# A hybrid attention and convolution layer in float32: four of 17 blocks of the product with V taken from rounded parts, and what moves with them

## The chip, the core and the metric

One core of a Trainium2 chip runs the whole layer in one launch. The metric is the device time of a run in microseconds, and a run is compared by its median. Engines are named as in the profile: PE (TensorE) with PEld (its weight loads), DVE (VectorE), ACT (ScalarE), POOL (GpSimd) and SP (SyncE, which here only issues DMAs).

## What is computed

The reference is one layer of a diffusion backbone: 2048 sample tokens (each attends to the 2048 sample keys and to 128 cached ones) and 128 prompt tokens, width 1024, four attention heads. What matters here is the attention of the sample tokens:

```python
s = jnp.einsum('bqhmd,bkhmd->bhmqk', qblk, k) * scale    # two maps m per head
p = jax.nn.softmax(s, axis=-1)
a = p[:, :, 0] - lam * p[:, :, 1]                        # 2176 keys = 17 blocks of 128
out = jnp.einsum('bhqk,bkhe->bqhe', a, v)                # v: 128 wide per head
```

Before it stand a normalization, adaLN modulation and one wide projection (q, k, v, gates, convolution branches), after it a gated normalization and the output projection.

## The kernel before

**Two kinds of matmul.** PE takes operands of type float32 or float32r. A float32r operand has to be a rounded value, so where the kernel wants float32 accuracy from it, it splits a number into a rounded high part and the remainder ("hi" and "lo") and makes three products, hi\*hi, hi\*lo and lo\*hi. The projections, the scores (`scores`, L926) and the output projection (`out_half`, L1087) work so. The transposes (`transposes`, L981) and the product with V (`product`, L989) take float32 operands. In the trace a float32 matmul of the product is two MATMUL records with a weight load each.

**Stages.** Projections (to about 780 us, the last ones being the convolution branches of four channel groups, `conv_unit`, in which POOL has nothing to do), the attention (about 830 to 1478 us), the output projection.

**The attention's steps.** One step belongs to one tile of 128 queries of one head; there are NT = 64. All four engines walk through the same numbered steps in loops of four (`Fori`, the first 8 or 16 written out), each in its own fixed order, and are held together by semaphores only. Work on one tile is spread over later steps: scores, maxima and exponentials of tile n in step n, its denominators and the combination of the two maps in step n + 1, its transposes in step n + 2, their last evacuation in step n + 3, the product with V in steps n + 4 and n + 5, for two tiles at a time, because the product takes 256 columns.

- PE, step n (four parts p = 0..3): scores of one of four pieces; in p = 1 and p = 2 also the last 384 keys of one map; the product of an earlier pair (`product`: half 0, nine key blocks, in even steps, half 1, eight blocks, in odd ones); four transposes of tile n - 2.
- DVE, step n: p = 0: maximum of 1024 scores (L1856), evacuation of four transposed blocks (keys 12 to 15) of tile n - 3 (`tr_dve`, L1823), then the denominators of tile n - 1: a multiplication of six numbers (L1874), a sum (L1878) and a reciprocal (L1882). p = 1: maximum of 768 scores and of 384 (`max_third`, L1842). p = 2: maximum of 1024, then `combine` (L1830), which adds the two maps over the first 1024 keys. p = 3: maxima of 384 and 768, and the smallest of them (`both_maxima`, L1742).
- ACT, step n: the exponentials (L1376, L1344), the scaling of the second map's first 1024 keys (`scale_first`, L1337; it waits for POOL's coefficients), the evacuation of the other transposed blocks (L1312), the product's result (`att_out`, L1320), and factors for the denominators (L1353).
- POOL, tile n (`factors`): two small multiplications that make the coefficients (L758, which waits for the reciprocal, and L760), six multiplications of 384 keys (L764 and L767 in turn), two additions of 576 keys (L773).

In steps 6 to 13 DVE also makes the low parts of the output weights (`wo_lo`, L1815), one per step, at the end of p = 1. At the start, DVE finishes the last convolution group inside step 1 (L1640 to L1662).

The kernel before calls the product with this wait in front of half 1: `pe.wait_ge(t_dve, n - 3)`.

Of the kernel before, what the change touches and what calls it, by code (L numbers as in the profile page):

```python
# [30 lines left out]
P = 128  # L31
# [6 lines left out]
H = 4  # L38
# [22 lines left out]
TGROUPS = [(0, 4), (4, 4), (8, 4), (12, 4), (16, 1)]  # L61
PIECES = [(0, 1024), (1024, 1792), (1792, KEYS)]
# [19 lines left out]
def hymba_layer(nc, a):  # L82
# [3 lines left out]
    for name, shape in (("k", [H, 2, P, KCOLS]), ("q", [H, 2, P, T]), ("v", [H, P, TILES, P]),  # L86
                        ("ga", [H, P, T]), ("cv", [H, 2, P, T]), ("att", [H, P, T])):
        spill[name] = nc.dram_tensor(f"spill_{name}", shape, F32, kind="Internal").ap()

    ctx = ExitStack()  # L90
    with ctx:
# [32 lines left out]
        with ExitStack() as ectx:  # L124
            qsl = sb("qsl", [P, 2, GW], F32R, ectx)
            blkr = sb("blkr", [P, P], F32R, ectx)
        cb = sb("cb", [P, D])
# [34 lines left out]
        with ExitStack() as bctx:  # L162
            kb = sb("kb", [P, 2, 2, KEYS], F32R, bctx)
            qb = sb("qb", [P, 4, 2, 2, P], F32R, bctx)
            sb("epad", [P, P], F32, bctx)
            e1 = sb("e1", [P, 2, KEYS], F32, bctx)
            e0 = sb("e0", [P, 4, KEYS], F32, bctx)
            with ExitStack() as kctx:
                kp = sb("kp", [P, H, T], F32R, kctx)
            at = sb("at", [P, 2, KT, 2 * P], F32, bctx)  # L170
            vb = sb("vb", [P, KT, P], F32, bctx)
            atto = sb("atto", [P, 2, 2 * P], F32, bctx)
            sb("spad", [P, 12 * 8 + 8 * H], F32, bctx)
            worw = sb("worw", [P, 2, DJ, P], F32, bctx)
            with ExitStack() as pctx:
                sb("vpad", [P, 6 * H * P], F32, pctx)
                sb("qpad", [P, 9 * H * P - P], F32, pctx)
                qp = sb("qp", [P, 2, 2 * H, P], F32R, pctx)
            wo = sb("wo", [P, DJ, 2, DJ, P], F32R, bctx)

# [165 lines left out]
        t_dve = sem("t_dve")  # L346
        pv_mm = sem("pv_mm")
# [39 lines left out]
        def f32(ap):  # L387
            return ap.bitcast(F32)
# [31 lines left out]
        def _(sp):  # L420
# [103 lines left out]
            def load_v(head, part):  # L524
                j0, j1 = (0, 9) if part == 0 else (9, KT - 1)
                sp.dma_start(vb[:, j0:j1], spill["v"][head, :, j0:j1]).then_inc(s_v[part], 16)
                if part == 1:
                    sp.dma_start(vb[:, KT - 1], a["cache_v"][:, head * P:(head + 1) * P]).then_inc(s_v[part], 16)
# [26 lines left out]

            def store_conv(f, tg):
                c0, c1 = behind(tg)
                sp.wait_ge(cvc, 4 + 6 * (NG * f + tg) + 6)
                for hl, src in ((0, chi), (1, clo)):
                    sp.dma_start(spill["cv"][f, hl, :, c0:c1], src[:, 0:c1 - c0]).then_inc(stored, 16)  # L560
# [6 lines left out]
            for f in range(H):  # L567
                c = CVC + CV * f
                for tg in range(NG):
# [7 lines left out]
                    if tg < 3:  # L577
                        for i in range(GATE_CUT[f] + 2 * tg, min(GATE_CUT[f] + 2 * tg + 2, GATE_CUT[f + 1])):
                            load_gate(i)
                    sp.wait_ge(z_used, CV0 + CV_UNITS * f + CV * tg + 1)  # L580
                    sp.dma_start(spill["ga"][f, :, c0:c0 + n], gs[:, 0:n]).then_inc(aux_stored, 16)
                    if tg == 3 and f + 1 < H:
                        sp.wait_ge(g_done, GATE_CUT[f + 1])
                        load_w(c + 5, 0)
                        load_w(c + 6, 1)
# [31 lines left out]
            load_q(3, 0, 3 * P)  # L617
            load_v(0, 0)
# [87 lines left out]
        def _(pool):  # L706
# [39 lines left out]
            qk_unit(H, 0, unit=False)  # L746

# [36 lines left out]
        def _(pe):  # L784
# [199 lines left out]
            def product(b, half, part):  # L984

                js = (range(0, 9), range(9, KT))[half]
                cut = (0, 2, 4, 6, 9) if half == 0 else (0, 2, 4, 6, 8)
                for i in range(cut[part], cut[part + 1]):
                    mm = pe.matmul(ps[:, 7, b * 2 * P:(b + 1) * 2 * P], vb[:, js[i]], at[:, b, js[i], :],  # L989
                                   start=(half == 0 and i == 0), stop=(half == 1 and i == len(js) - 1))  # L990
                if part == 3:
                    mm.then_inc(pv_mm, 1)

            def step(it, t, sc=True, tr=True, tr_last=True, pv=True):
                n = 4 * it + t
                for p in range(4):
# [18 lines left out]
                    if pv:  # L1015
                        half = t % 2
                        b = t // 2
                        if p == 0:
                            pe.wait_ge(s_v[half], (32 if half else 16) * ((it + 3) // 4))
# [449 lines left out]
        def _(dve):  # L1469
# [347 lines left out]
            def tr_dve(n, t):  # L1817

                j0, cnt = TGROUPS[3]
                dve.wait_ge(t_mm, 5 * n + 4)  # L1820
                if t % 2 == 0:
                    wait(dve, pv_mm, n - 2)
                dve.tensor_copy(at[:, t // 2, j0:j0 + cnt, (t % 2) * P:(t % 2 + 1) * P],  # L1823
                                trbank(3).rearrange("p (j q) -> p j q", j=cnt)).then_inc(t_dve, 1)
# [20 lines left out]
            def step(it, t, sc=True, den=True, comb=True, tr_last=True):  # L1845
                n = 4 * it + t
                b = t % 2
                for p in range(4):
# [23 lines left out]
                    if p == 0 and den:  # L1872
# [3 lines left out]
                    if p == 0 and den:  # L1876
# [3 lines left out]
                    if p == 0 and den:  # L1880
# [178 lines left out]
```

## Time and profile before

| what | value |
|---|---|
| runs | 1669.56 us median of 3 (1669.47 to 1671.62) |
| profiled execution | 1670.42 us, span 1668.6 us, granted clock 0.992 |
| PE busy | 1629.1 us (98%) |
| DVE, ACT, POOL busy over the span | 1018.3 (61%), 873.2 (52%), 765.5 (46%) |
| attention steps, 1000 to 1200 us: DVE, ACT, POOL busy | 167.83, 179.19, 186.55 of 200 us |

How to read it: the busy shares over the span mix stages with very different loads (POOL has no work at all in the convolution stage). A PE that is shown as busy need not be at its peak, since its matmuls overlap in the records: how fast it goes is seen from the distance between the starts of its matmuls. Lines are those of the kernel before.

### The profile page before, as it was taken

How to read it: one execution, taken by the hardware profiler on the slowest of the kernel's cores; microseconds unless marked ns; L12 is line 12 of the kernel's file. 1: busy time of each engine (PE TensorE's matmuls, PEld its weight loads, DVE VectorE, ACT ScalarE, POOL GpSimd, SP SyncE). 2: the span in 40 equal slices, each digit the busy share in tenths (PEclk: the TensorE clock that was granted, in tenths of full speed). 3: DMA queues.
4: the chain of work that ended last, by engine and by line, in shares of the span. 5: the costliest groups of instructions: out<-in, count | busy, mean ns of one | idle time of the engine just before them, and what ended most of it. 6: DMA issues, size and time to landing. Idle time of an engine off the chain costs nothing.

```text
span 1668.6 us, 25622 instructions
## 1 busy us (share of the span) xinstructions
PE 1629.1 (98%) x8476; PEld 1460.1 (88%) x8476; DVE 1018.3 (61%) x1613; ACT 873.2 (52%) x1827; POOL 765.5 (46%) x807
## 2 busy tenths in 40 slices
PE   4999999999999999999989999999999999999999
PEld 2888999999999999999968888888888888889999
DVE  4553666663343344333389988888888888745442
ACT  4664666640010100100279989989889898823320
POOL 0002898960000000000079999999999999800000
PEclk8999999999999999999979999999999999999999
DMA  9662323342131231124152223113211211265441
GB/s 366 221 206 101 120 101 110 112 145 84 58 108 54 71 107 53 59 68 121 40 132 87 84 51 93 38 35 85 64 31 35 65 31 50 76 211 182 177 158 49
DMA packets 127232, 168.47 MB, mean 101 GB/s; under 512 B 10816, under 2 KB 113728, under 8 KB 126272
## 3 DMA queue, kind: packets, MB, share of 16 engines
q1 hardware_dynamic: 122032, 163.19, 30.3%
q10 hardware_dynamic: 5136, 4.46, 0.8%
q8 instruction: 36, 0.59, 0.2%
q14 instruction: 28, 0.23, 0.0%
HBM read 117.54 MB, written 50.07 MB: 100 GB/s over the span
## 4 chain that ended last, share of the span: by engine, by line
PE 85%; DMA 4%; DVE 3%; ACT 3%; SPq 2%; issue 2%; POOL 1%; DVEq 0%; POOLq 0%; ACTq 0%
PE ps L808 39%; PE ps L926 14%; PE ps L989 13%; PE ps L1087 11%; PE ps L981 7%; DMA scr<-in_xtok 1%; DMA raw<-in_w_in 1%; DMA xt<-in_xtok 1%; DVE stt L1856 1%; DMA out_y<-yo 1%; ACT scr L1175 1%; SPq L535 1%; PE ps L860 0%; PE ps L861 0%; SPq L430 0%
## 5 line engine op out<-in xcount | busy, mean ns | idle before, releaser
L808 PE MATMUL ps<-hT,w 128*128 128x448 f32 (+1 forms) x3360 | 677.3, 361 | 0.3 <-DVE w L1500 0.3
L808 PEld LDWEIGHTS ps<-hT,w 128*128 128x128 f32 x3360 | 621.7, 188 | 48.2 <-DVE w L1500 1.1
L926 PE MATMUL ps<-kb,qb 128*128 (+2 forms) x1276 | 321.3, 381 | 8.5 <-ACT e L1376 4.0
L1856 DVE TENSOR_REDUCE stt<-ps 128x1 f32<-128x1024 f32 x252 | 273.6, 1086 | 58.8 <-PE ps L926 58.4
L1376 ACT ACTIVATE e<-ps,stt 128x1024 f32<-128x1024 f32 x252 | 255.6, 1014 | 61.1 <-DVE stt L1856 54.6
L989 PE MATMUL ps<-at,vb 128*128 128x256 f32 x1088 | 276.7, 381 | 0.8 <-ACT atto L1320 0.5
L758 POOL TENSOR_TENSOR stt<-stt,lamc 128x2 f32<-128x2 f32 x64 | 12.5, 195 | 505.8 <-DVE stt L1882 505.8
L926 PEld LDWEIGHTS ps<-kb,qb 128*128 128x128 f32 x1276 | 217.8, 192 | 26.5 <-issue 7.1
L989 PEld LDWEIGHTS ps<-at,vb 128*128 128x128 f32 x1088 | 199.0, 190 | 29.0 <-ACT atto L1320 3.2
L764 POOL TENSOR_TENSOR e<-e,stt 128x384 f32<-128x384 f32 x192 | 212.5, 1107 | 5.0
L1282 ACT ACTIVATE scr<-ps 128x448 f32<-128x448 f32 (+1 forms) x40 | 20.9, 532 | 311.5 <-PE ps L808 311.5
L773 POOL TENSOR_TENSOR e<-e 128x576 f32<-128x576 f32 x128 | 180.7, 1430 | 0.0
L981 PE MATMUL ps<-cst,e 128*128 128x128 f32 x1088 | 172.3, 275 | 2.2 <-DVE e L1830 0.7
L767 POOL TENSOR_TENSOR e<-e,stt 128x384 f32<-128x384 f32 x192 | 173.7, 905 | 0.0
L981 PEld LDWEIGHTS ps<-cst,e 128*128 128x128 f32 x1088 | 137.6, 142 | 35.4 <-issue 3.5
L1312 ACT ACTIVATE at<-ps 128x512 f32<-128x512 f32 (+1 forms) x256 | 131.6, 515 | 9.4 <-PE ps L981 9.4
L727 POOL TENSOR_TENSOR qx<-qx,scr 128x448 f32<-128x448 f32 (+1 forms) x40 | 45.2, 1129 | 169.8 <-DVE qx L1597 165.7
L808 PE MATMUL ps<-w,hT 128*128 128x512 f32 x408 | 97.5, 399 | 8.2 <-DVE hT L1550 8.1
L1830 DVE SCALAR_TENSOR_TENSOR e<-e,stt 128x1024 f32<-128x1024 f32 x64 | 90.4, 1413 | 19.5 <-ACT e L1337 19.5
L1087 PE MATMUL ps<-mixa,wo 128*128 128x448 f32 (+1 forms) x480 | 101.1, 360 | 0.0
L1087 PE MATMUL ps<-mixc,wo 128*128 128x448 f32 (+1 forms) x480 | 100.9, 360 | 0.0
L808 PEld LDWEIGHTS ps<-w,hT 128*128 128x128 f32 x408 | 77.5, 192 | 25.2 <-DVE hT L1550 7.8
(161 smaller groups left out, 1751.8 us busy)
## 6 DMA issues: line engine op xcount, KB each, us to landing
raw<-in_w_in SPq DMA_DIRECT2D x32, 512.0 KB, 4.4
qb<-spill_q SPq DMA_DIRECT2D x256, 64.0 KB, 2.3
scr<-in_xT SPq DMA_DIRECT2D x8, 1024.0 KB, 6.1
raw<-in_w_gate SPq DMA_DIRECT2D x16, 512.0 KB, 4.4
spill_k<-scr SPq DMA_DIRECT2D x32, 224.0 KB, 2.2
spill_q<-scr SPq DMA_DIRECT2D x32, 224.0 KB, 2.2
mixc<-spill_cv SPq DMA_DIRECT2D x8, 896.0 KB, 7.9
xr<-in_xT SPq DMA_DIRECT2D x4, 1792.0 KB, 13.2
```

Source lines behind the costliest of these rows:

```text
L764: pool.tensor_tensor(e1[:, b, k0:k1], e1[:, b, k0:k1], stt[:, b, 7, 3 + c:4 + c].to_broadcast([P, k1 - k0]), ALU.mult)\
L767: pool.tensor_tensor(e0[:, t, k0:k1], e0[:, t, k0:k1], stt[:, b, 7, c:c + 1].to_broadcast([P, k1 - k0]), ALU.mult)\
L773: add = pool.tensor_tensor(e0[:, t, k0:k1], e0[:, t, k0:k1], e1[:, b, k0:k1], ALU.add)
L808: mm = pe.matmul(out, slot_of(l, j), rhs_of(r, j), start=(i == 0 and j == 0), stop=(i == 2 and j == DJ - 1))
L926: mm = pe.matmul(out[:, c0 - k0:c1 - k0], qb[:, t, ver, m], keys, start=(ver == 0), stop=(ver == 1))
L981: mm = pe.transpose(trbank(g)[:, i * P:(i + 1) * P], e0[:, t, (j0 + i) * P:(j0 + i + 1) * P], ident)
L989: mm = pe.matmul(ps[:, 7, b * 2 * P:(b + 1) * 2 * P], vb[:, js[i]], at[:, b, js[i], :], start=(half == 0 and i == 0), stop=(half == 1 and ...
L1087: mm = pe.matmul(ps[:, k % 4, 0:n], wo[:, o, l, j + H * (1 - half)], part[:, r, j, 0:n], start=(half == 0 and i == 0 and j == 0), stop=(ha ...
L1312: act.activation(at[:, t // 2, j0:j0 + cnt, (t % 2) * P:(t % 2 + 1) * P], trbank(g).rearrange("p (j q) -> p j q", j=cnt), ACT.Copy).then_i ...
L1376: act.activation(dst[:, PIECES[c][0]:PIECES[c][1]], pair(c), ACT.Exp, bias=stt[:, b, 0, 3 * m + c:3 * m + c + 1], accum_out=stt[:, b, 1, 3 ...
L1830: dve.scalar_tensor_tensor(e0[:, t, k0:k1], e0[:, t, k0:k1], stt[:, t % 2, 7, 0:1], e1[:, t % 2, k0:k1], ALU.mult, ALU.add).then_inc(a_rea ...
L1856: dve.tensor_reduce(stt[:, b, 0, 3 * m + c:3 * m + c + 1], pair(c), AX.X, ALU.max, negate=True).then_inc(mx_done, 1)
```

## The change

Three things change together.

1. The product with V takes key blocks 12 to 15 (SB0 = 12, SB = 4) from rounded parts: three float32r matmuls of 256 columns in place of one float32 matmul. DVE's evacuation of these blocks writes the rounded high part `ath` instead of `at`, and a second instruction subtracts it from the transposed block in PSUM into the low part `atl`. The order of the blocks changes (HALVES), so that all four lie in half 0, and PE's wait for DVE's evacuation moves to p = 2 of half 0. `atl` has one buffer, so the evacuation of the next pair waits for one more product (`pv_mm`).
2. V's parts are made in the last channel group of the convolution stage: per head one load of four blocks, POOL's copy (high) and subtraction (low), two stores. In the attention, a head's V comes as four DMAs and a small one instead of two and a small one.
3. The denominators (L1874, L1878, L1882) move in DVE's order from p = 0 to p = 1, behind the second maximum and `max_third`, in front of `wo_lo`.

```diff
+SB0, SB = TGROUPS[3]
+HALVES = ([0, 1, 2, 3, 12, 4, 13, 14, 15], [5, 6, 7, 8, 9, 10, 11, 16])
+CUTS = ((0, 2, 4, 6, 9), (0, 2, 4, 6, 8))
...
             def load_v(head, part):
-                j0, j1 = (0, 9) if part == 0 else (9, KT - 1)
-                sp.dma_start(vb[:, j0:j1], spill["v"][head, :, j0:j1]).then_inc(s_v[part], 16)
...
+                if part == 0:
+                    sp.dma_start(vb[:, 0:5], spill["v"][head, :, 0:5]).then_inc(s_v[0], 16)
+                    for hl in range(2):
+                        sp.dma_start(f32(vhl[:, hl]), spill["vs"][hl, head]).then_inc(s_v[0], 16)
+                else:
+                    sp.dma_start(vb[:, 5:SB0], spill["v"][head, :, 5:SB0]).then_inc(s_v[1], 16)
+                    sp.dma_start(vb[:, KT - 1], a["cache_v"][:, head * P:(head + 1) * P]).then_inc(s_v[1], 16)
...
+            def load_parts(head):
+                if head == 0:
+                    sp.wait_ge(g_done, GATE_CUT[H])
+                    for i in range(2):
+                        sp.wait_ge(v_stored[i], 16 * ((TILES + 1 - i) // 2))
+                wait(sp, vs_stored, 32 * head)
+                sp.dma_start(vraw[:], spill["v"][head, :, SB0:SB0 + SB]).then_inc(vs_in, 16)
+
+            def store_parts(head):
+                sp.wait_ge(vs_lo, head + 1)
+                for hl in range(2):
+                    sp.dma_start(spill["vs"][hl, head], f32(vhl[:, hl])).then_inc(vs_stored, 16)
...
+                    if f == H - 1 and tg < H:
+                        load_parts(tg)
                     sp.wait_ge(z_used, CV0 + CV_UNITS * f + CV * tg + 1)
                     sp.dma_start(spill["ga"][f, :, c0:c0 + n], gs[:, 0:n]).then_inc(aux_stored, 16)
+                    if f == H - 1 and tg < H:
+                        store_parts(tg)
...
+            for head in range(H):
+                pool.wait_ge(vs_in, 16 * (head + 1))
+                pool.tensor_copy(vhl[:, 0], vraw[:]).then_inc(vs_hi, 1)
+                pool.wait_ge(vs_hi, head + 1)
+                pool.tensor_tensor(vhl[:, 1], vraw[:], f32(vhl[:, 0]), ALU.subtract).then_inc(vs_lo, 1)
...
             def product(b, half, part):
+                    if SB0 <= j < SB0 + SB:
+                        pe.matmul(out, vhl[:, 0, j - SB0], ath[:, b, j], start=first, stop=False)
+                        pe.matmul(out, vhl[:, 0, j - SB0], atl[:, j - SB0], start=False, stop=False)
+                        mm = pe.matmul(out, vhl[:, 1, j - SB0], ath[:, b, j], start=False, stop=last)
+                    else:
+                        mm = pe.matmul(out, vb[:, j], at[:, b, j, :], start=first, stop=last)
...
-                                pe.wait_ge(t_dve, n - 3)
+                        if p == 2 and half == 0:
+                            pe.wait_ge(t_dve, n - 2)
                         product(b, half, p)
...
                 if t % 2 == 0:
-                    wait(dve, pv_mm, n - 2)
-                dve.tensor_copy(at[:, t // 2, j0:j0 + cnt, (t % 2) * P:(t % 2 + 1) * P],
-                                trbank(3).rearrange("p (j q) -> p j q", j=cnt)).then_inc(t_dve, 1)
+                    wait(dve, pv_mm, n - 1)
+                cols = slice((t % 2) * P, (t % 2 + 1) * P)
+                src = trbank(3).rearrange("p (j q) -> p j q", j=cnt)
+                dve.tensor_copy(ath[:, t // 2, j0:j0 + cnt, cols], src).then_inc(t_dvh, 1)
+                dve.wait_ge(t_dvh, n + 1)
+                dve.tensor_tensor(atl[:, :, cols], src, f32(ath[:, t // 2, j0:j0 + cnt, cols]), ALU.subtract).then_inc(t_dve, 1)
...
-                    if p == 0 and den:
+                    if p == (1 if sc else 0) and den:
                         dve.wait_ge(f_done, n)
```

## Rows read from the trace of the kernel before

**Rows 1.** Windows: busy us (count) of PE, PEld, DVE, ACT, POOL; convolutions, attention.

```profile
645.00:670.00 25.00, 25.00 (x123) 22.72 (x122) 8.94 (x15) 1.09 (x2) 0.00 (x0) 1.00 0.16 57
1000.00:1200.00 200.00, 200.00 (x1135) 177.56 (x1134) 167.83 (x252) 179.19 (x411) 186.55 (x210) 1.00 0.26 65
```

**Rows 2.** POOL's first instruction of a tile, L758, 985 to 1436 us.

```profile
L758 POOL TENSOR_TENSOR stt<-stt,lamc x47: 194/195/197, 990.6 to 1429.3; 128x2 f32<-128x2 f32 x47
```

**Rows 3.** Timeline of POOL, one tile (start, length, instruction, idle before).

```profile
1206.65 2.79 POOL L773 TENSOR_TENSOR e<-e 128x576 f32<-128x576 f32 x2
1209.94 0.19 POOL L758 TENSOR_TENSOR stt<-stt,lamc 128x2 f32<-128x2 f32 x1 [0.49 <-DVE stt L1882]
1210.21 0.20 POOL L760 TENSOR_TENSOR stt<-stt 128x6 f32<-128x6 f32 x1
1210.49 0.83 POOL L764 TENSOR_TENSOR e<-e,stt 128x384 f32<-128x384 f32 x1
1211.28 0.83 POOL L767 TENSOR_TENSOR e<-e,stt 128x384 f32<-128x384 f32 x1
...
1213.63 1.81 POOL L764 TENSOR_TENSOR e<-e,stt 128x384 f32<-128x384 f32 x1
...
1219.47 0.20 POOL L758 TENSOR_TENSOR stt<-stt,lamc 128x2 f32<-128x2 f32 x1 [0.50 <-DVE stt L1882]
```

**Rows 4.** Timeline of DVE, and of ACT's scaling L1337, in the same step.

```profile
1207.20 1.22 DVE L1856 TENSOR_REDUCE stt<-ps 128x1 f32<-128x1024 f32 x1 [0.38 <-PE ps L926]
1208.34 0.68 DVE L1823 COPY at<-ps 128x512 f32<-128x512 f32 x1
1208.94 0.52 DVE L1874 TENSOR_TENSOR stt<-stt 128x6 f32<-128x6 f32 x1
...
1209.79 0.96 DVE L1856 TENSOR_REDUCE stt<-ps 128x1 f32<-128x768 f32 x1
1210.67 0.55 DVE L1842 TENSOR_REDUCE stt<-ps 128x1 f32<-128x384 f32 x1
...
1212.23 1.14 ACT L1337 ACTIVATE e<-e,stt 128x1024 f32<-128x1024 f32 x1
...
1213.41 1.35 DVE L1830 SCALAR_TENSOR_TENSOR e<-e,stt 128x1024 f32<-128x1024 f32 x1 [0.28 <-ACT e L1337]
...
1216.20 0.16 DVE L1742 TENSOR_REDUCE stt<-stt 128x2 f32<-128x6 f32 x1
```

**Rows 5.** Timeline of PE, a part of the same step.

```profile
1211.71 1.02 PE L989 MATMUL ps<-at,vb 128*128 128x256 f32 x4
1212.57 0.60 PE L981 MATMUL ps<-cst,e 128*128 128x128 f32 x4
```

**Rows 6.** Timeline of PE, float32r matmuls of 128 columns, and what follows.

```profile
785.36 2.00 PE L885 MATMUL ps<-kp,qp 128*128 128x128 f32 x16 [0.17 <-DMA kp<-spill_k]
787.20 1.45 PE L808 MATMUL ps<-hT,w 128*128 128x448 f32 x6
```

**Rows 7.** Waits of PE's weight loads, 985 to 1436 us: total, times, longest.

```profile
PEld ps L989 <- ACT atto L1320: 2.6, 12, 0.2
```

**Rows 8.** Timeline, projection stage: a DVE instruction with one input in PSUM beside POOL.

```profile
300.68 0.62 DVE L1577 TENSOR_TENSOR qsl<-ps,qsh 128x448 fp32r<-128x448 f32 x1 [0.90 <-ACT qsh L1212]
300.97 1.16 POOL L729 TENSOR_TENSOR qx<-qx,scr 128x448 f32<-128x448 f32 x1
```

**Rows 9.** L758 from 889 to 972 us, and DVE's `wo_lo`.

```profile
L758 POOL TENSOR_TENSOR stt<-stt,lamc x9: 185/194/197, 889.6 to 971.5; 128x2 f32<-128x2 f32 x9
...
L1815 DVE TENSOR_TENSOR wo<-worw,wo x8: 1214/1308/1309, 890.8 to 962.7; 128x1024 fp32r<-128x1024 f32 x8
```

**Rows 10.** Timeline of POOL around 910 us and at the attention's third tile.

```profile
907.40 2.79 POOL L773 TENSOR_TENSOR e<-e 128x576 f32<-128x576 f32 x2
910.16 0.18 POOL L758 TENSOR_TENSOR stt<-stt,lamc 128x2 f32<-128x2 f32 x1
...
861.03 0.20 POOL L758 TENSOR_TENSOR stt<-stt,lamc 128x2 f32<-128x2 f32 x1 [1.27 <-DVE stt L1882]
```

More of the change, by code:

```diff
@@ L86, in hymba_layer @@
     for name, shape in (("k", [H, 2, P, KCOLS]), ("q", [H, 2, P, T]), ("v", [H, P, TILES, P]),
-                        ("ga", [H, P, T]), ("cv", [H, 2, P, T]), ("att", [H, P, T])):
+                        ("vs", [2, H, P, SB, P]), ("ga", [H, P, T]), ("cv", [H, 2, P, T]), ("att", [H, P, T])):
         spill[name] = nc.dram_tensor(f"spill_{name}", shape, F32, kind="Internal").ap()
@@ L126, in hymba_layer @@
             blkr = sb("blkr", [P, P], F32R, ectx)
+        with ExitStack() as vctx:
+            vhl = sb("vhl", [P, 2, SB, P], F32R, vctx)
+        with ExitStack() as vctx:
+            sb("vgap", [P, SB, P], F32, vctx)
+            vraw = sb("vraw", [P, SB, P], F32, vctx)
         cb = sb("cb", [P, D])
@@ L169, in hymba_layer @@
                 kp = sb("kp", [P, H, T], F32R, kctx)
+            with ExitStack() as hctx:
+                ath = sb("ath", [P, 2, KT, 2 * P], F32R, hctx)
             at = sb("at", [P, 2, KT, 2 * P], F32, bctx)
@@ L179, in hymba_layer @@
             wo = sb("wo", [P, DJ, 2, DJ, P], F32R, bctx)
+            atl = sb("atl", [P, SB, 2 * P], F32R, bctx)
         with ExitStack() as cctx:
@@ L346, in hymba_layer @@
         t_dve = sem("t_dve")
+        t_dvh = sem("t_dvh")
+        vs_in = sem("vs_in")
+        vs_hi = sem("vs_hi")
+        vs_lo = sem("vs_lo")
+        vs_stored = sem("vs_stored")
         pv_mm = sem("pv_mm")
@@ L524, in load_v @@
             def load_v(head, part):
-                j0, j1 = (0, 9) if part == 0 else (9, KT - 1)
-                sp.dma_start(vb[:, j0:j1], spill["v"][head, :, j0:j1]).then_inc(s_v[part], 16)
-                if part == 1:
-                    sp.dma_start(vb[:, KT - 1], a["cache_v"][:, head * P:(head + 1) * P]).then_inc(s_v[part], 16)
+                if part == 0:
[5 more added lines that the diff above has]
+                    sp.dma_start(vb[:, KT - 1], a["cache_v"][:, head * P:(head + 1) * P]).then_inc(s_v[1], 16)
             def load_prompt():
@@ L617, in _ @@
             load_q(3, 0, 3 * P)
+            sp.wait_ge(vs_stored, 32 * H)
             load_v(0, 0)
@@ L984, in product @@
             def product(b, half, part):
-                js = (range(0, 9), range(9, KT))[half]
-                cut = (0, 2, 4, 6, 9) if half == 0 else (0, 2, 4, 6, 8)
+                js, cut = HALVES[half], CUTS[half]
+                out = ps[:, 7, b * 2 * P:(b + 1) * 2 * P]
                 for i in range(cut[part], cut[part + 1]):
-                    mm = pe.matmul(ps[:, 7, b * 2 * P:(b + 1) * 2 * P], vb[:, js[i]], at[:, b, js[i], :],
-                                   start=(half == 0 and i == 0), stop=(half == 1 and i == len(js) - 1))
+                    j, first, last = js[i], half == 0 and i == 0, half == 1 and i == len(js) - 1
+                    if SB0 <= j < SB0 + SB:
[4 more added lines that the diff above has]
+                        mm = pe.matmul(out, vb[:, j], at[:, b, j, :], start=first, stop=last)
                 if part == 3:
@@ L1018, in step @@
                         if p == 0:
-                            pe.wait_ge(s_v[half], (32 if half else 16) * ((it + 3) // 4))
+                            pe.wait_ge(s_v[half], (32 if half else 48) * ((it + 3) // 4))
                             if half == 0:
@@ L1875, in step @@
                             .then_inc(fz_done, 1)
-                    if p == 0 and den:
+                    if p == (1 if sc else 0) and den:
                         dve.wait_ge(fz_done, n)
@@ L1879, in step @@
                             .then_inc(den_done, 1)
-                    if p == 0 and den:
+                    if p == (1 if sc else 0) and den:
                         dve.wait_ge(den_done, n)
```

## The prediction

> **What bounds the kernel now.** I read the windows by stage first. In the attention steps PE is busy for the whole stretch, and DVE, ACT and POOL for 84, 90 and 93% of it [rows 1]. So four engines are close together, and a busy PE alone doesn't say who sets the pace. The wait list of PE's weight loads adds little: one wait for ACT's evacuation `att_out`, 12 times in 450 us, 0.2 us each, that is once in four steps [rows 7].
>
> The timelines decide it. POOL starts a tile 47 times between 990.6 and 1429.3 us [rows 2], 438.7 / 46 = 9.54 us apart. Within a tile it has no gap but one: 0.49 or 0.50 us in front of L758, waiting for DVE's reciprocal [rows 3]. And why is the reciprocal late? L1874 multiplies six numbers and is shown with 0.52 us; it starts at 1208.94 and ends at 1209.46, right behind POOL's additions, which end at 1206.65 + 2.79 = 1209.44 [rows 3, 4]. L1874 has both inputs in SBUF, as all of POOL's instructions have, and it does not run until POOL's instruction is through. So POOL's cycle is closed in itself: 9.04 us of work, then 0.49 us in which DVE makes the denominators, which can't start before POOL has ended. Its sum, 9.53, is the pace of all engines. The 0.2 us of [rows 7] is PE held back to it. PE alone would need 9.49 (9.54 less 0.2 / 4).
>
> The same lock works the other way: `combine` waits for POOL's multiplication and then holds POOL's next one, 1.81 in place of 0.83 us [rows 3, 4]. This 0.98 is part of the 9.04.
>
> **The change part by part.**
>
> *The product.* A float32 block costs two records: four records take from 1211.71 to 1212.57 [rows 5], 0.43 us a block. Float32r with 256 columns doesn't occur in the trace. From below: 128 columns go at (787.20 - 785.36) / 16 = 0.115 us [rows 6]. From above: 448 columns at 25 / 123 = 0.203 [rows 1]. By columns alone, 256 would be 0.203 x 256 / 448 = 0.116, the same as the lower bound; I take 0.118. Three make 0.354, 0.077 less than 0.431. Four blocks per pair of steps: 0.31 us less per two steps, PE's own need falls from 9.49 to 9.34 us. At the upper bound, 0.61 a block, it would rise by 0.36 a step to 9.85 and PE would set the pace; 256 columns can hardly cost as much as 448, so I leave that end out. The Trainium skill (TensorE: Matmul & The Clock Gate, Back-to-back issue gap) gives 262 cycles for 256 columns, 0.109 us; by it a pair of steps would save 0.42. No run shows it yet.
>
> As POOL sets the pace, this term counts for nothing in the loop: what covers it is PE's wait, and without POOL's cycle it would be worth 32 x 0.31 = 9.9 us.
>
> *The low part.* The copy stays as it is (0.68), the subtraction comes on top: 512 elements, one input in PSUM, one in SBUF. The nearest row is L1577 with 448 elements, 0.62 us [rows 8]; scaled 0.69. It ends at 301.30, in the midst of POOL's L729 (300.97 to 302.13), not behind its end as L1874 does, so the port isn't taken. It must wait for the copy to land, so from copy to next maximum DVE needs 0.72 + 0.61 = 1.33. The Trainium skill (SBUF — State Buffer, Who interferes with whom) says that DVE instructions with at most one SBUF input don't contend with GpSimd and that ones with two do, the later one waiting; the trace agrees with both halves.
>
> *The denominators moved.* Would POOL's cycle shorten? Only if L1874 came before POOL's last addition began. Follow the new chain from the end of L1874 (1209.46): coefficients ready +0.95 (1210.41, rows 3); ACT's scaling, now waiting for them, takes 1.14 [rows 4], done at about +2.1; `combine` waits for POOL's second multiplication (1211.28 + 0.83 = 1212.11, +2.65) and ends 1.13 after one (1213.41 + 1.35 = 1214.76, against 1213.63, where the multiplication that it waited for makes way for the next): +3.78. From there to `both_maxima` 1.44 and its 0.16 [rows 4]: +5.38. Then the next first maximum 1.14, the two evacuations 1.33, the maxima 0.88 and 0.47 (each from start to start, the last 0.55 less 0.08 of overlap) [rows 4]: L1874 is issued at +9.20. POOL ends at +0.48 + 9.04 = +9.52. So L1874 again waits, about 0.3 us, and again releases POOL 0.49 us after its end. **The cycle stays 9.53.** DVE now has 0.3 us to spare where it had more; ACT is not later than before by more than it idles.
>
> *The stretch with `wo_lo`.* Eight cycles, 889.6 to 971.5, take 81.9 us [rows 9], 10.24 each: `wo_lo` holds one more POOL instruction (+1.0), but in every second step L1874 falls between POOL's two additions and POOL goes on without a gap, as at 907.40 + 2.79 = 910.19 against 910.16 [rows 10]. After the change `wo_lo` stands directly behind the reciprocal. Its 1.2 us [rows 9] hold the port just when L758 wants it: +1.0, with `combine` as before; and since L1874 now comes 0.3 us in front of POOL's end, the gapless steps are gone. 8 x (9.54 + 1.0) = 84.3: **+2.4 us**. Bounds: 0 if POOL gets in first, +5 if ACT's chain adds.
>
> *The start.* POOL's third tile starts at 861.03 after 1.27 us of waiting [rows 10]; from there the closed cycle counts every delay. The denominators come later by the low part and two maxima, 0.6 + 0.88 + 0.47 = 2.0 us; but in step 1 POOL no longer collides with DVE's last convolution work, which DVE gains. Between 0 and +2.0 I take **+1.0**.
>
> *The end.* The last tiles wait for POOL's chain, so a later POOL is a later end. One half 0 of the product lies behind it on PE alone, **-0.3**, and the last L1874, with no scores in front of it, can slip between POOL's instructions, **-0.5** (the gap of [rows 3]).
>
> *V's parts.* In the last convolution group POOL is idle and DVE busy for 36% of a stretch [rows 1]; four copies and subtractions (576 elements in 2.79 / 2 = 1.4 us on POOL [rows 10], a bound for both), four loads and eight stores lie under PE's matmuls, 120 of them (24 us) per token group. SP's wait for the low part stands behind a wait for PE's first unit, 24 x 0.203 = 5 us, about what load and POOL need. 0. If it isn't covered, SP's next store comes a few us late, with a group's time to spare. The two more DMAs per head have a whole step.
>
> **Sum**: +2.4 + 1.0 - 0.3 - 0.5 = +2.6, against the profiled execution's 1670.42: 1673.0. That one stood 0.9 above the median of the runs, so **1672.2 us**.
>
> **Rivals.**
>
> *PE sets the pace after all* (it ends faster). For it: PE 100% busy, waits of 2.6 us only. Against it: L1874's length is always what is missing to POOL's end. It decides from the point at which POOL can cycle in under 9.4 us, that is when L1874 is issued more than 1.4 us (an addition) before POOL's end. Then -9.9 + 1.0 = about 1661. Chance 0.15.
>
> *DVE's chain is a bit longer than its spare 0.3 us*: it now sets the pace, say 0.1 to 0.2 per step over 50 steps: +5 to +10, 1677 to 1682. Chance 0.11.
>
> *`combine` misses POOL's boundary*, because ACT is over 0.5 us later: one more multiplication, 0.79; L1874 comes at +9.99, after POOL's end, the cycle is about 10.0: 48 x 0.5 = +24, 1696. Chance 0.06.
>
> *The low part does take the port*, +0.6 per cycle, 48 times: about 1700. [rows 8] speak against it. Chance 0.06.
>
> **How the numbers follow.** My forecast has 0.62. A measurement here can tell 0.2%, 3.3 us, from no change. With the bounds of its terms the forecast spans 1668 to 1677; the sum at +2.6 lies just under the 3.3, so I give 0.26 to its part above them and 0.36 to the part within. So faster 0.15, same 0.36, slower 0.11 + 0.06 + 0.06 + 0.26 = 0.49. The range takes in the first two rivals: 1661 to 1680; the likeliest case alone: 1668 to 1677.
>
> **What would show it.** L758 starts 9.53 to 9.55 us apart in the loop, with a gap of 0.49 in front; L1874 stays longer than 0.24 us and ends with POOL's addition; L989's and the new matmuls' starts lie 0.115 to 0.12 apart; PE has waits of 0.15 to 0.2 us a step that it didn't have. In the `wo_lo` stretch eight cycles of 10.5. POOL's third tile starts at about 862. The prediction is wrong if POOL's cycle falls under 9.5 (first rival) or exceeds 9.6; in the latter case L1874 with 0.16 to 0.24 us, no longer locked, means that DVE or ACT is the bound.

## The result and the profile after

The changed kernel takes 1675.37 us (median of 7 runs, 1672.59 to 1675.76) against 1669.56 (7 runs, 1668.82 to 1671.62). The ratio of the runs is 1.0025, 95% interval 1.0016 to 1.0034: slower by a quarter of a percent, a little more than the 0.2% that the prediction named as what can be told. A repeat beside other runs (e4 below) gave 1674.46 and a ratio of 1.0020 (1.0011 to 1.0029). By the medians the change costs 5.8 us in the first comparison and 3.8 in the second.

Lines have moved. POOL: L758 is now L801, L760 L803, L764 L807, L767 L810, L773 L816. DVE: the maxima L1856 and L1842 are L1908 and L1894, the evacuation L1823 is L1874 (high part) and L1876 (low part), the denominators L1874, L1878, L1882 are L1926, L1930, L1934, `combine` is L1882, `both_maxima` L1791, `wo_lo` L1864. PE: the product is L1034 to L1036 (parts) and L1038 (float32). So that no line is mistaken, the first instruction of the denominators is called *the multiplication* from here.

POOL's first instruction of a tile, over the same stretch as [rows 2], and in the stretch of `wo_lo` as [rows 9]; the columns are shortest, median and longest duration in ns, and the first and last start:

```profile
L801 POOL TENSOR_TENSOR stt<-stt,lamc x47: 194/195/197, 992.8 to 1432.6; 128x2 f32<-128x2 f32 x47
...
L801 POOL TENSOR_TENSOR stt<-stt,lamc x9: 195/1096/1097, 890.2 to 973.7; 128x2 f32<-128x2 f32 x9
```

439.8 / 46 = 9.56 us a tile, after 9.54; and 83.5 us for the eight cycles with `wo_lo`, after 81.9. POOL's timeline at one usual tile and at one in four:

```profile
1209.38 2.80 POOL L816 TENSOR_TENSOR e<-e 128x576 f32<-128x576 f32 x2
1212.68 0.19 POOL L801 TENSOR_TENSOR stt<-stt,lamc 128x2 f32<-128x2 f32 x1 [0.50 <-DVE stt L1934]
...
1222.29 0.20 POOL L801 TENSOR_TENSOR stt<-stt,lamc 128x2 f32<-128x2 f32 x1 [0.58 <-DVE stt L1934]
...
1231.84 0.20 POOL L801 TENSOR_TENSOR stt<-stt,lamc 128x2 f32<-128x2 f32 x1 [0.49 <-DVE stt L1934]
```

DVE's timeline for the same tiles:

```profile
1209.17 0.68 DVE L1874 CAST ath<-ps 128x512 fp32r<-128x512 f32 x1
1209.88 0.69 DVE L1876 TENSOR_TENSOR atl<-ps,ath 128x512 fp32r<-128x512 f32 x1
1210.49 0.95 DVE L1908 TENSOR_REDUCE stt<-ps 128x1 f32<-128x768 f32 x1
1211.36 0.55 DVE L1894 TENSOR_REDUCE stt<-ps 128x1 f32<-128x384 f32 x1
1211.82 0.38 DVE L1926 TENSOR_TENSOR stt<-stt 128x6 f32<-128x6 f32 x1
...
1217.87 1.22 DVE L1908 TENSOR_REDUCE stt<-ps 128x1 f32<-128x1024 f32 x1 [0.34 <-issue]
...
1221.66 0.16 DVE L1926 TENSOR_TENSOR stt<-stt 128x6 f32<-128x6 f32 x1
```

The multiplication is issued at 1211.82, before POOL's additions end (1209.38 + 2.80 = 1212.18), and ends with them, at 1212.20: the lock of [rows 3, 4] is as it was. One tile in four it is issued at 1221.66, with only 0.06 us to go, and takes 0.16. It is late because DVE's first instruction of a pass of its loop of four steps starts 0.34 us late, "issue" by the profile (time in which the engine waited for nothing that the profile shows). Then POOL's gap is 0.55 to 0.60 instead of 0.49.

PE, as [rows 5], and its weight loads' waits, as [rows 7]:

```profile
1205.29 0.28 PE L1034 MATMUL ps<-ath,vhl 128*128 128x256 f32 x1
1205.41 0.28 PE L1035 MATMUL ps<-atl,vhl 128*128 128x256 f32 x1
1205.53 0.28 PE L1036 MATMUL ps<-ath,vhl 128*128 128x256 f32 x1
1205.64 0.28 PE L1034 MATMUL ps<-ath,vhl 128*128 128x256 f32 x1
```

```profile
PEld ps L1024 <- ACT e L1393: 5.7, 22, 0.4
PEld ps L1024 <- issue: 4.5, 12, 0.4
PEld ps L1038 <- ACT atto L1369: 2.6, 12, 0.2
```

The parts start 0.117 us apart, 0.35 a block where a float32 block took 0.43. PE's saving is there, and it has gone into waiting: 12.8 us in the stretch where the wait for ACT had been 2.6. That is 0.27 a step, 9.56 - 0.27 = 9.29 of its own. Of the 12.8, 4.5 are "issue", once in four steps; if that is PE's own time and no wait for another engine, its need is 9.38. So it lies between 9.3 and 9.4.

### The profile page after: what moved, and what is told of

Its sections match the earlier page's. It is cut to its first block, busy times and chain, and to the rows that moved or that the text cites. A ratio compares the mean times of both kernels' runs of the same rounds, so it can differ in the third digit from the quotient of the medians.

```text
span 1670.8 us, 25984 instructions
## 1 busy us (share of the span) xinstructions
PE 1625.8 (97%) x8604; PEld 1453.6 (87%) x8604; DVE 1054.0 (63%) x1677; ACT 884.9 (53%) x1827; POOL 774.9 (46%) x815
## 4 chain that ended last, share of the span: by engine, by line
PE 80%; DVE 7%; DMA 4%; ACT 3%; issue 2%; POOL 2%; SPq 1%; DVEq 0%; POOLq 0%; ACTq 0%
PE ps L851 40%; PE ps L969 11%; PE ps L1136 11%; PE ps L1038 9%; PE ps L1024 6%; DVE stt L1908 2%; DVE e L1882 1%; DMA scr<-in_xtok 1%; DMA raw<-in_w_in 1%; ACT e L1386 1%; DMA xt<-in_xtok 1%; DVE stt L1894 1%; DMA out_y<-yo 1%; PE ps L1036 1%; PE ps L1034 1%
## 5 line engine op out<-in xcount | busy, mean ns | idle before, releaser
L969 PE MATMUL ps<-kb,qb 128*128 (+2 forms) x1276 | 318.9, 378 | 10.0 <-ACT e L1425 4.4
L1908 DVE TENSOR_REDUCE stt<-ps 128x1 f32<-128x1024 f32 x252 | 273.1, 1084 | 14.0 <-PE ps L969 6.6
L969 PEld LDWEIGHTS ps<-kb,qb 128*128 128x128 f32 x1276 | 215.5, 190 | 29.4 <-issue 9.5
L807 POOL TENSOR_TENSOR e<-e,stt 128x384 f32<-128x384 f32 x192 | 220.6, 1149 | 5.0
L1038 PE MATMUL ps<-at,vb 128*128 128x256 f32 x832 | 218.2, 383 | 1.0 <-ACT atto L1369 0.5
L787 POOL CAST vhl<-vraw 128x512 fp32r<-128x512 f32 x4 | 3.6, 892 | 427.9 <-DMA vraw<-spill_v 427.9
L816 POOL TENSOR_TENSOR e<-e 128x576 f32<-128x576 f32 x128 | 178.8, 1416 | 0.0
L1038 PEld LDWEIGHTS ps<-at,vb 128*128 128x128 f32 x832 | 148.7, 189 | 20.0 <-ACT atto L1369 3.1
L810 POOL TENSOR_TENSOR e<-e,stt 128x384 f32<-128x384 f32 x192 | 159.3, 829 | 0.0
L764 POOL TENSOR_TENSOR qx<-qx,scr 128x448 f32<-128x448 f32 (+1 forms) x40 | 45.2, 1129 | 170.8 <-DVE qx L1646 166.7
L1882 DVE SCALAR_TENSOR_TENSOR e<-e,stt 128x1024 f32<-128x1024 f32 x64 | 99.6, 1557 | 30.0 <-ACT e L1386 29.9
```

The costliest lines, as they stand in the source:

```text
L807: pool.tensor_tensor(e1[:, b, k0:k1], e1[:, b, k0:k1], stt[:, b, 7, 3 + c:4 + c].to_broadcast([P, k1 - k0]), ALU.mult)\
L810: pool.tensor_tensor(e0[:, t, k0:k1], e0[:, t, k0:k1], stt[:, b, 7, c:c + 1].to_broadcast([P, k1 - k0]), ALU.mult)\
L816: add = pool.tensor_tensor(e0[:, t, k0:k1], e0[:, t, k0:k1], e1[:, b, k0:k1], ALU.add)
L969: mm = pe.matmul(out[:, c0 - k0:c1 - k0], qb[:, t, ver, m], keys, start=(ver == 0), stop=(ver == 1))
L1038: mm = pe.matmul(out, vb[:, j], at[:, b, j, :], start=first, stop=last)
L1882: dve.scalar_tensor_tensor(e0[:, t, k0:k1], e0[:, t, k0:k1], stt[:, t % 2, 7, 0:1], e1[:, t % 2, k0:k1], ALU.mult, ALU.add).then_inc(a_rea ...
```

## Where the time went

By POOL's starts in the two profiled executions (1672.59 against 1670.42 us; spans 1670.8 against 1668.6):

| stretch | before | after | difference |
|---|---|---|---|
| start of POOL's third tile | 861.03 | 861.53 | +0.50 |
| the next eleven tiles, eight of them with `wo_lo` | 110.50 | 112.14 | +1.64 |
| the 48 tiles from there | 457.77 | 458.93 | +1.16 |
| the last two cycles | 19.05 | 18.53 | -0.52 |
| POOL's last start to the end of the span | 220.25 | 219.67 | -0.58 |

The first row is not the denominators' doing alone. PE's first scores behind its last projection (L926 before, L969 after) start at:

```profile
833.00 0.85 PE L926 MATMUL ps<-kb,qb 128*128 128x384 f32 x4
```

```profile
833.84 0.85 PE L969 MATMUL ps<-kb,qb 128*128 128x384 f32 x4
```

and in the second profile of the changed kernel (e4):

```profile
832.71 0.85 PE L969 MATMUL ps<-kb,qb 128*128 128x384 f32 x4
```

The changed kernel is 0.84 us behind the kernel before there in one execution and 0.29 ahead in the other, and from there to POOL's third tile (861.03; 861.53; 861.41) it needs 0.34 us less and 0.67 more. So executions differ by more than the row, and the cost at the start isn't told from nothing. V's parts, made before this point, have no cost that these profiles show.

The profiled execution is the shortest of the seven; the median is 2.8 us above it. The last section has a difference of that size that the profiles show, between executions and not between kernels.

## The experiments

Pace is the mean distance between POOL's first instructions of two tiles, about 1000 to 1400 us. Each group of runs stood beside its own runs of the kernel before, whose medians were 1670.67 (e1 to e4), 1671.10 (e5 to e8), 1670.09 (e9 to e11) and 1671.61 us (e12). A pace is that of one profiled execution.

| run | median us | ratio to before (95%) | pace us |
|---|---|---|---|
| e1, before + denominators moved | 1672.38 | 1.0007 (0.9998 to 1.0015) | 9.54 |
| e2, after, denominators back in p = 0 | 1679.95 | 1.0049 (1.0036 to 1.0063) | 9.63 |
| e3, after, denominators before the evacuation | 1692.01 | 1.0133 (1.0116 to 1.0150) | 9.88 |
| e4, after again | 1674.46 | 1.0020 (1.0011 to 1.0029) | 9.56 |
| e5, before, POOL 0.46 us less | 1666.89 | 0.9967 (0.9954 to 0.9979) | 9.49 |
| e6, after, POOL 0.46 us less | 1663.98 | 0.9949 (0.9936 to 0.9963) | 9.43 |
| e7, after, second addition cut 448 + 128 | 1668.71 | 0.9981 (0.9970 to 0.9992) | 9.51 |
| e8, after, 192 keys from POOL to ACT | 1670.29 | 0.9988 (0.9979 to 0.9996) | 9.53 |
| e9, after, multiplications 288, 480, 384 | 1677.36 | 1.0037 (1.0023 to 1.0051) | 9.60 |
| e10, e9 + second addition cut 320 + 256 | 1668.51 | 0.9982 (0.9973 to 0.9991) | 9.47 |
| e11, before + both cuts of e10 | 1669.85 | 0.9995 (0.9986 to 1.0004) | 9.55 |
| e12, e9 + second addition cut 416 + 160 | 1668.47 | 0.9985 (0.9976 to 0.9994) | 9.50 |

**e1: only the denominators moved.**

```diff
-                    if p == 0 and den:
+                    if p == (1 if sc else 0) and den:
```

> The kernel before with only the denominators moved behind the second maxima; the product and its evacuation stay as they were. Theory (POOL's closed cycle): L1874 is issued about 1.0 us before POOL's additions end, still inside the second addition (1.4), so it waits for its end and the steady pace stays 9.54 us; the wo_lo stretch costs +1 to +2.5, the start 0 to +1, no late L1874 in any fourth step: 1669 to 1673 us. Rival (the change's loss is DVE's longer chain with the low part): this kernel has no low part, so it is equal to before, 1669.5 us, also in the wo_lo stretch.

The pace is 9.54, the `wo_lo` stretch 83.4 us (+1.5), the third tile starts at 861.67. So the theory's terms came, and none of the fourth steps is late. One size was off: the multiplication is issued 0.3 to 0.6 us before POOL's additions end, not 1.0, since on this chain DVE waits for PE's scores, 0.44 us in front of the maximum of 1024 and in some tiles 0.30 in front of that of 768. It is still locked and takes 0.33 to 0.62 us. The stretch loses its gapless steps without a low part; the rival, which had this kernel equal there, falls, though the interval of the whole time reaches 1.

**e2 and e3: the changed kernel with the denominators earlier.** e2 has `p == 0` as the kernel before, e3 puts them in front of the evacuation as well:

```diff
+                    if p == 0 and den:
+                        dve.wait_ge(f_done, n)
...
                     if p == 0 and tr_last:
                         tr_dve(n - 1 - S_TR, (t - 1 - S_TR) % 4)
-                    if p == (1 if sc else 0) and den:
```

> The changed kernel with the denominators back in p = 0, behind the low part. Theory: in the changed kernel PE needs only 9.34 us a step; what holds it is that the multiplication for the denominators falls inside POOL's second addition. Back in p = 0 the chain from its end to its next issue is about 7.9 us, 1.7 us before POOL's end, that is before the second addition begins (1.4): it slips between the two, POOL's gap of 0.49 goes, and the pace falls toward PE's 9.34: 1660 to 1664 us. Rival A (the pace is not POOL's closed cycle but DVE's or ACT's chain): the low part stands in front of the denominators and makes them later, 1672 to 1700 us. Rival B: it still falls into the second addition: pace 9.54, 1668 to 1671 us, with the start and the wo_lo stretch as before.

> The changed kernel with the denominators in p = 0 in front of the evacuation and its low part. Theory: issued a further 1.3 us earlier, about 3 us before POOL's end: before or at the start of the first addition, so it slips in at a boundary, POOL's gap goes, the pace is PE's 9.34 to 9.40: 1659 to 1664 us. Rival A (chain): equal to the changed kernel, 1673 to 1676. Rival B: it waits for ACT's factors and holds DVE; then DVE is late and the pace stays 9.5 or more: 1668 to 1680 us.

My theory of these two was wrong, and rival A right in e2; e3, at 1692, lies outside all the ranges given for it. The multiplication is no longer locked in either (0.15 to 0.17 us), and both are slower. In e2 it takes 9.40 us from its end to its next issue, where I had expected 7.9. DVE in e2, one step:

```profile
1205.99 0.96 DVE L1908 TENSOR_REDUCE stt<-ps 128x1 f32<-128x768 f32 x1
...
1209.61 1.35 DVE L1882 SCALAR_TENSOR_TENSOR e<-e,stt 128x1024 f32<-128x1024 f32 x1 [0.51 <-ACT e L1386]
...
1212.60 1.23 DVE L1908 TENSOR_REDUCE stt<-ps 128x1 f32<-128x1024 f32 x1
1213.74 0.68 DVE L1874 CAST ath<-ps 128x512 fp32r<-128x512 f32 x1
1214.46 0.69 DVE L1876 TENSOR_TENSOR atl<-ps,ath 128x512 fp32r<-128x512 f32 x1
1215.07 0.15 DVE L1926 TENSOR_TENSOR stt<-stt 128x6 f32<-128x6 f32 x1
...
1215.55 0.96 DVE L1908 TENSOR_REDUCE stt<-ps 128x1 f32<-128x768 f32 x1
```

and ACT between the first two:

```profile
1206.99 0.90 ACT L1425 ACTIVATE e<-ps,stt 128x768 f32<-128x768 f32 x1 [0.99 <-DVE stt L1908]
...
1207.88 0.57 ACT L1393 ACTIVATE e<-ps,stt 128x384 f32<-128x384 f32 x1
...
1208.44 1.14 ACT L1386 ACTIVATE e<-e,stt 128x1024 f32<-128x1024 f32 x1
```

This is a second closed chain, and I had not seen it: ACT's scaling stands in ACT's order behind the exponentials of the second piece, and these wait for DVE's maximum of 768. From that maximum (1205.99) over exponentials, scaling, `combine`, the maxima, the evacuation and the denominators to the next maximum of 768 (1215.55) it is 9.56 us without a gap, more at a loop's turn (9.85), and POOL, whose coefficients were ready at 1206.6, isn't on it. The low part is 0.61 of it and the denominators 0.48. In the changed kernel's order the denominators are off this chain, and by estimate it is 9.56 - 0.48 = 9.08, under POOL's 9.54. So, given the low part, the move is worth 5.5 us (e2 against e4). In e3 evacuation and low part are put off by the denominators, and PE waits for them as well (for L1876, 13.9 us in 45 waits between 985 and 1436). e3 is 0.25 us a step above e2. `combine`, which is on the chain, takes 1.55 us there on average and 1.35 in e2, which is 0.20; that this is the 0.25 wasn't tested.

So the two halves of the change don't add up: the move alone costs 1.7 us by the medians (e1, with an interval that reaches 1), the product and its low part alone 9.3 (e2), both together 3.8 (e4).

**e4: the changed kernel once more.**

> The changed kernel once more, for a second profile of it and for the comparison with the others on one chip: 1672 to 1676 us. Theory: the steady pace is 9.54 to 9.56, and the difference of 2.5 us between its own runs is either in how many steps have a late denominator multiplication or in the start.

Its profile has the same pace, the same one late tile in four and the same `wo_lo` stretch (83.5 us). The spread of its runs, 1672.32 to 1676.65, isn't explained by these.

**e5 and e6: less work for POOL, in either kernel.**

```diff
-                for i, (k0, k1) in enumerate(((1024, 1600), (1600, KEYS))):
+                for i, (k0, k1) in enumerate(((1216, 1600), (1600, KEYS))):
```

> The kernel before with POOL's first addition cut from 576 to 384 keys (keys 1024 to 1215 are not added, so this is left out of the result): 0.46 us less of POOL's work a tile, nothing else. Theory: POOL's closed cycle falls from 9.54 to 9.07, so PE sets the pace with its own 9.49: only 0.05 us a step less, about -2 to -3 us, 1667 to 1669 us. Rival (POOL sets the pace and PE has much room): 9.07 to 9.2 a step, -16 to -22 us, 1648 to 1654.

> The changed kernel with the same cut of POOL's first addition (keys 1024 to 1215 are not added). Theory: POOL's cycle falls to 9.07, the chain of coefficients, ACT, combine and DVE needs 9.16 + 0.16 = 9.32, PE 9.34: the pace goes to 9.34 to 9.40, 0.15 to 0.2 us a step less than now: 1664 to 1667 us, that is 3 to 5 us under the kernel before with the same cut, where the uncut pair stands the other way. Rival (PE's saving isn't there, or DVE is the bound at 9.54): no less than the kernel before with the cut, 1669 or more.

Both within 0.2 us of the theory's ranges. In the kernel before POOL then works 8.63 us of a step and waits the rest for a multiplication that is no longer locked, and the pace falls by 0.04 only; PE's waits between 985 and 1436 us are gone:

```profile
PEld ps L989 <- ACT atto L1320: 0.2, 1, 0.2
```

That is PE's own 9.49. The changed kernel with the cut is 2.9 us under this one (its median against the other's, of one group of runs; six runs of 1665.38 to 1668.06 and five of 1662.90 to 1666.93, which overlap), where the uncut ones of e4's group stand 3.8 the other way. Its pace of 9.43 is below the 9.49 that PE needs in the kernel before: PE's saving becomes time when POOL's cycle makes way, 2.9 us of the 9.9 that the prediction gave for it. It reaches 9.43, not 9.34. The steps are 9.43, 9.62, 9.32 and 9.32: 9.32 is the chain of coefficients, ACT, `combine` and DVE, without a gap, and in the two longer ones, around the loop's turn, DVE waits 0.17 and 0.35 us on it for PE's scores.

**e7: a boundary for the multiplication.** The same work, only POOL's second addition in two instructions:

```diff
-                for i, (k0, k1) in enumerate(((1024, 1600), (1600, KEYS))):
-                    pool.wait_ge(e1_done, 3 * n + 2 + i)
-                    pool.wait_ge(e0_done, 3 * n + 2 + i)
+                for i, (k0, k1) in enumerate(((1024, 1600), (1600, KEYS - P), (KEYS - P, KEYS))):
+                    if i < 2:
+                        pool.wait_ge(e1_done, 3 * n + 2 + i)
+                        pool.wait_ge(e0_done, 3 * n + 2 + i)
```

> The changed kernel with POOL's second addition (576 keys) cut in two, 448 and 128 keys; no work is left out. Theory (the lock): the multiplication for the denominators is issued 0.36 us before POOL's additions end; a boundary 0.31 us before the end lets it in there, so the coefficients come 0.2 to 0.3 us earlier, less the two holds of POOL's last addition (0.16) and of one more instruction (0.03): pace 9.34 to 9.45 in the steps in which it is early enough, 9.54 in the others: 1664 to 1671 us. Rival (the multiplication waits for POOL's results or for the queue to be empty, not for the port): nothing changes, 1674 to 1676.

POOL (three additions) and the multiplication, missed and caught:

```profile
1208.18 2.95 POOL L817 TENSOR_TENSOR e<-e 128x576 f32<-128x576 f32 x3
1211.62 0.20 POOL L801 TENSOR_TENSOR stt<-stt,lamc 128x2 f32<-128x2 f32 x1 [0.49 <-DVE stt L1935]
...
1227.58 2.94 POOL L817 TENSOR_TENSOR e<-e 128x576 f32<-128x576 f32 x3
1230.65 0.20 POOL L801 TENSOR_TENSOR stt<-stt,lamc 128x2 f32<-128x2 f32 x1
```

```profile
1210.72 0.43 DVE L1927 TENSOR_TENSOR stt<-stt 128x6 f32<-128x6 f32 x1
...
1230.02 0.16 DVE L1927 TENSOR_TENSOR stt<-stt 128x6 f32<-128x6 f32 x1
```

The additions are merged in these rows; the last one of the first tile by itself:

```profile
1210.67 0.46 POOL L817 TENSOR_TENSOR e<-e 128x128 f32<-128x128 f32 x1
```

At 1210.72 the last addition had begun 0.05 us before: the multiplication waits for its end, POOL's gap is 0.49, the tile 9.70. At 1230.02 it comes at the boundary, takes 0.16, the gap is 0.13, the tile 9.33. Two of four tiles are caught and two missed. The `wo_lo` stretch falls to 81.8 us. One added instruction, with no work taken away, makes the changed kernel 6 us faster (1668.71 against e4's 1674.46, in another group of runs) and faster than the kernel before; the rival is out.

**e8: work from POOL to ACT.**

```diff
+AK = 192
...
+                    ka = k0 + AK if k0 == 1024 else k0
...
+                    if i == 0:
+                        pool.wait_ge(e1b_done, n + 1)
...
                                scale=stt[:, t % 2, 7, 3:4]).then_inc(e1a_done, 1)
+                act.activation(e1[:, t % 2, 1024:1024 + AK], e1[:, t % 2, 1024:1024 + AK], ACT.Copy,
+                               scale=stt[:, t % 2, 7, 4:5]).then_inc(e1b_done, 1)
```

> The changed kernel with 192 of POOL's 384 keys of the first multiplication of e1 scaled by ACT right behind its own scaling; no work is left out. Theory: POOL's work falls by 0.39 to 8.65, its cycle to 9.15; combine, which waited for POOL's boundary, comes earlier too; ACT has 0.49 us idle in its step and takes about 0.39: PE's 9.34 sets the pace: 1662 to 1666 us, under the kernel before. Rival (ACT is the bound, the added 0.39 lies on its chain): pace 9.6 or more, 1676 to 1690.

In between, at 1670.29 outside both ranges. POOL waits 0.5 to 0.9 us per tile for the denominators, unlocked, so its cycle is no longer the bound, but the pace is 9.53: DVE waits up to 0.7 us for PE's scores, and PE waits 9.0 us between 985 and 1436, 6.1 of them for ACT and 2.9 "issue". ACT's instruction, 0.44 us, takes part of the gain back, it seems; which chain sets the 9.53 wasn't found.

**e9 to e12: another boundary for `combine`, and then for the multiplication.**

```diff
-PARTS = [(1, 1024, 1408), (1, 1408, 1792), (2, 1792, KEYS)]
+PARTS = [(1, 1024, 1312), (1, 1312, 1792), (2, 1792, KEYS)]
```

> The changed kernel with POOL's six multiplications cut at other keys: 288, 480 and 384 keys in place of three times 384; no work is left out. Theory: ACT's scaling ends 1.11 us after POOL's first multiplication begins, and combine then waits for POOL's boundary at 1.57; now a boundary comes at 1.18, so combine takes 1.28 in place of 1.55 and DVE's chain is 0.3 to 0.4 shorter. The multiplication for the denominators is issued 0.7 us before POOL's end and still waits for it: pace 9.54, and the late one in every fourth step is gone: 1 us less, 1672 to 1675 us. Rival (DVE's chain sets the pace): 0.3 us a step less, 1658 to 1662.

> The changed kernel with the cut of the multiplications at 288, 480 and 384 keys and POOL's second addition cut in 320 and 256 keys. Theory: the multiplication for the denominators is issued 0.7 us before POOL's end, the boundary lies 0.6 before it, so it is let in there in most steps, and POOL's gap of 0.49 goes to about 0: POOL's cycle 9.2 to 9.3, DVE's chain 8.9 to 9.0, PE's 9.34 sets the pace: 1660 to 1666 us, below both kernels. Rival (PE's saving is not there): 9.49 a step, 1668 to 1671.

> The kernel before (float32 product, denominators in p = 0) with the same two cuts of POOL's instructions. Theory: POOL's cycle falls here too, but PE needs 9.49: pace 9.49 to 9.51, 1667 to 1670 us, 3 to 7 us above the changed kernel with the same cuts. Rival (POOL alone was the matter and PE has room): the same time as the changed kernel with the cuts, 1660 to 1666.

> As the changed kernel with both cuts of POOL's instructions, but with the second addition cut in 416 and 160 keys in place of 320 and 256; no work is left out. Theory (the lock): with 256 keys the multiplication for the denominators came 0.82 us before POOL's end in one step and was let in, and 0.52 to 0.69 before it in the next and missed the boundary at 0.6. A boundary at 0.39 before the end is caught from all of these: POOL's gap falls to about 0.05 in every step, its cycle to 9.32, and PE's 9.34 sets the pace: 1661 to 1666 us. Rival (something else holds every second step, so that a step of 9.2 is paid back by one of 9.7): the mean pace stays 9.47 and the time 1667 to 1670.

Three of the four theories missed. e9, at 1677.36, is above its 1672 to 1675; e10 (1668.51) and e12 (1668.47) are above theirs and inside the ranges of their rivals; e11 (1669.85) is inside its own, but with a pace of 9.55 for 9.49 to 9.51.

e9: `combine` takes 1.28 us in place of 1.55 and the multiplication is issued 0.37 to 0.69 us before POOL's end, never late, yet the pace is 9.60 where e4's is 9.56 (the intervals of the two ratios overlap). DVE's chain was shortened and the pace did not fall with it, so it doesn't set it; it rose, because POOL's own work rose from 9.05 to 9.10: the held multiplication now has 480 keys and takes 2.02 us, 1.04 more than the one after it, which isn't held (0.98), where the hold had been 0.98. 9.10 and the gap of 0.50 are the pace of 9.60.

e10: tiles of 9.20 (caught at 0.82 us before the end, no gap) and of 9.74 (missed) in turn.

e12: I had expected that 160 keys would catch all; tiles of 9.26, 9.25, 9.74, 9.74. In the missed ones the multiplication comes 0.04 us or less behind the last addition's start: I read this as the closed chain's own doing: a caught step brings POOL forward, and the next multiplication is late against it. That is argued, not tested; the rival of e12, that a short step is paid back by a long one whatever the boundary, stands. e10's rival, that PE's saving isn't there, falls by the pace: 9.47, and 9.43 in e6, are below the 9.49 that PE needs in the kernel before.

e11 against e10: the same cuts are worth nothing in the kernel before and 6 us in the changed one, but the two differ by 1.3 us only, less than I had given. In e11 one tile in four is caught (9.14) and three are missed (9.68), and its pace of 9.55 is above PE's 9.49. So the lock still holds this kernel, and the pair doesn't show what PE's saving is worth; e5 and e6 do.

e7, e10 and e12 beat both kernels: 1668.5 to 1668.7 us, 0.15 to 0.19% under the kernel before, with intervals that end below 1, as does e8's at 0.12%. All four differences are below the 0.2% that the prediction named as what can be told, so they rest on these intervals alone.

## Why the prediction was right

The forecast was 1672.2 us (+2.6 by the profiled execution, 1673.0); it measured 1675.4, in the range and in the likeliest case's own range of 1668 to 1677, and its profiled execution 1672.59. What held is the mechanism of the loop: POOL's cycle with the lock sets the pace, and PE's saving turns into waits (e7, e5 and e6). The size is less good: the median moved by 5.8 us (3.8 in the repeat) where the sum has 2.6. Step by step:

- *The pace stays 9.53; L1874 again waits about 0.3 us.* Shown: 0.36 us, released with POOL's additions; the chain from its end to its next issue is 9.17 for 9.20, and 9.46 at the loop's turn. The pace is 9.56, just outside the 9.53 to 9.55 that were to show it.
- *PE's term counts for nothing.* Shown: 0.117 us a matmul for 0.118 (not the 0.109 given beside it), PE's need 9.3 to 9.4 for 9.34, and 0.27 us a step of waits, 0.21 more than before for 0.15 to 0.2; e5 against e6 gives back 2.9 us of the term's 9.9.
- *The low part doesn't take the port.* Shown: 0.69 us as forecast, beside POOL's addition of 2.80.
- *The `wo_lo` stretch, +2.4.* It is +1.6: the gapless steps are gone, but a step takes 10.43, not 10.54. I had added 1.0 for `wo_lo` to the steady cycle; POOL's work grew by 0.89 (9.94 for 9.05).
- *The start, +1.0.* The row is +0.5, but the changed kernel was 0.84 late already at the end of the projections in this execution, and 0.29 early in e4's. The term isn't resolved, and that it fits is luck.
- *The end, -0.3 and -0.5.* -0.58 and -0.52. The last multiplication did slip between two instructions of POOL.
- *V's parts, 0.* No cost is seen at the end of the projections.
- *Rival "DVE's chain is longer than its spare".* Not in the sum, but a part of it came: the spare of 0.36 doesn't cover the 0.3 us at the loop's turn, so one tile in four is 0.07 longer: about 0.9 of the +1.16, the rest being 0.007 us in each of the other tiles. This is the term that I missed, and it stood in the trace of before as steps of L1874 whose lengths differ by 0.25 us within a group of four.

The sum was met in the profiled executions (+2.17 for +2.6) with terms off in both directions, and this is in part luck. The remaining 2.8 us between the profiled execution and the median are not in any of its steps, and where they come from stays open.

The Trainium skill (SBUF — State Buffer, Who interferes with whom) has the later of two contenders wait. e7 agrees, down to 0.05 us: a multiplication issued 0.05 us behind the start of POOL's last addition waits for its end, one issued 0.04 us ahead of it runs.

## What to carry to other kernels

Before you cost a cheaper instruction, find the closed chain that sets the pace, and then the second one right behind it: here three stand close (POOL with its lock 9.54 us, PE 9.49 or 9.3, the ring of DVE and ACT 9.08 by estimate, or 9.56 with the denominators on it), and a gain in one is worth only the distance to the next. Where a tiny DVE instruction with two inputs in SBUF waits behind a long one of POOL, cut the long one so that a boundary comes just after the small one is issued, and measure: this was worth 6 us in the changed kernel (e7), such cuts gained nothing in the kernel before (e11), and no cut caught the small one in every step. And where the ring through the next engine is the longest, put small work behind the instruction that feeds that engine, not in front of it: 0.48 us of denominators in front of a maximum cost 5.5 us in all once the low part was there (e2 against e4). Without the low part the same move gained nothing (e1).

## What the runs showed of the hardware that was not expected

The output projection runs at one of two speeds with a granted clock of 1.00 in both. Windows of 1500 to 1600 us, kernel before and then e10 (PE, PEld, DVE, ACT and POOL busy with counts, clock, DMA share, GB/s):

```profile
1500.00:1600.00 100.00, 100.00 (x495) 92.83 (x495) 51.08 (x85) 33.69 (x62) 0.00 (x0) 1.00 0.49 176
```

```profile
1500.00:1600.00 100.00, 100.00 (x485) 90.83 (x485) 48.72 (x80) 31.00 (x58) 0.00 (x0) 1.00 0.51 179
```

Twelve matmuls of 448 columns take 2.43 us from start to start in the first and 2.48 in the second, neither with a wait. Over the stage it adds up to about 2.5 us:

```profile
1527.59 2.60 PE L1087 MATMUL ps<-mixa,wo 128*128 128x448 f32 x12
1530.02 2.59 PE L1087 MATMUL ps<-mixc,wo 128*128 128x448 f32 x12
```

```profile
1527.71 2.64 PE L1137 MATMUL ps<-mixc,wo 128*128 128x448 f32 x12
1530.19 2.64 PE L1137 MATMUL ps<-mixa,wo 128*128 128x448 f32 x12
```

Four of the 14 profiled executions (e1, e2, e10, e12) have it, the kernel before and the changed one don't, and e9, whose code for this stage is the same as e10's, doesn't have it either. What it depends on stays open. It has the size of the changed kernel's 2.8 us between profile and median; that this is the reason wasn't shown, as the other runs have no profile.
